# A decoder layer on one core: the feed-forward region of SBUF begins at another byte

## The reference

```python
x = x + 0.5 * swiglu(rmsnorm(x, n1), g1, u1, d1)          # 2048 -> 5632 -> 2048
h = rmsnorm(x, nm)
z = h @ w_in                                              # split by columns
x = x + concat([hgrn2_mix(z...), nsa_mix(z...)]) @ w_out  # 8 recurrent heads; 16 attention heads
x = x + mem_cross_attn(rmsnorm(x, nx), rmsnorm(mem, nmem), wq, wk, wv, wo)
x = x + 0.5 * swiglu(rmsnorm(x, n2), g2, u2, d2)
return rmsnorm(x, final_norm)
```

## The kernel before

| tile | where | remainder before |
| --- | --- | --- |
| `x`, `xT`, `w_raw`, `w_hi`, `w_lo`, `silu_gate`, `ff_hidden`, `kxT`, `ident` | ahead of `ff` | 128 |
| `ffT_hi`, `ffT_lo`, `mem_x`, `z_qf`, `z_ig`, `att`, level mask | in the region | 128 |
| `z_n` | in the region | 128 for tokens 0 to 127, 320 for the others |
| `qT`, `kT`, `prob0`, `probT` | in the region | 0 |
| `prob1` | in the region | 256 |
| `blk_hi`, `blk_lo` | in the region | 256 and 0 at the start, then steps of 264 bytes |

## Time and profile before

### The profile page before, as it was taken

How to read it: one execution, slowest core, us unless ns; L and a number is a source line. 1 busy time by engine, 2 the same in 40 slices (tenths; PEclk the granted TensorE clock), 3 DMA queues, 4 the chain that set the end, 5 groups by cost and what they waited for, 6 DMA issues and landing times.

```text
span 2136.0 us, 25561 instructions
## 1 busy us (share of the span) xinstructions
PE 2073.8 (97%) x9679; PEld 1727.3 (81%) x9679; DVE 1118.2 (52%) x1400; ACT 940.6 (44%) x1181; POOL 0.2 (0%) x4
## 2 busy tenths in 40 slices
PE   6999999999999999999999999799999999999997
PEld 5888888888888888878888987678888888888886
DVE  4544554445544445676567455454544545444444
ACT  6544444444444445454454244444444444444443
POOL 0000000000000000000000000000000000000000
PEclk8999999999999999999998699899999999999999
DMA  6666666666666566675540055256666666666563
GB/s 220 182 189 190 192 186 187 188 192 189 187 191 193 188 191 184 188 218 156 158 148 1 1 195 177 82 168 190 185 191 189 188 192 185 203 196 196 191 193 128
DMA packets 194343, 372.23 MB, mean 174 GB/s; under 512 B 12904, under 2 KB 15456, under 8 KB 194144
## 3 DMA queue, kind: packets, MB, share of 16 engines
q1 hardware_dynamic: 190176, 366.62, 57.0%
q10 hardware_dynamic: 4096, 4.64, 0.6%
HBM read 369.11 MB, written 2.10 MB: 174 GB/s over the span
## 4 chain that ended last, share of the span: by engine, by line
PE 94%; DVE 3%; ACT 2%; ACTq 1%; issue 1%; DVEq 0%
PE psum L1203 87%; PE psum L1214 2%; PE psum L1485 1%; PE psum L1439 1%; PE psum L1307 1%; PE psum L1407 0%; PE psum L1420 0%; ACT w_hi L423 0%; DVE xT_lo L781 0%; ACT xT_hi L446 0%; ACT silu_gate L453 0%; DVE att L1090 0%; DVE w_lo L745 0%; PE psum L1386 0%; ACTq L476 0%
## 5 line engine op out<-in xcount | busy, mean ns | idle before, releaser
L745 DVE TENSOR_TENSOR w_lo<-w_raw,w_hi 128x1024 fp32r<-128x1024 f32 x696 | 850.9, 1225 | 906.6 <-ACT w_hi L423 905.3
L423 ACT ACTIVATE w_hi<-w_raw 128x1024 fp32r<-128x1024 f32 x696 | 736.5, 1060 | 1028.6 <-PE psum L1203 1016.1
L1203 PE MATMUL psum<-w_hi,xT_hi 128*128 128x512 f32 (+1 forms) x1824 | 713.1, 391 | 7.5 <-DVE xT_lo L781 4.9
L1203 PE MATMUL psum<-w_hi,xT_lo 128*128 128x512 f32 (+1 forms) x1824 | 708.2, 388 | 0.0
L1203 PE MATMUL psum<-w_lo,xT_hi 128*128 128x512 f32 (+1 forms) x1824 | 708.1, 388 | 0.0
L1203 PEld LDWEIGHTS psum<-w_hi,xT_hi 128*128 128x128 f32 x1824 | 343.1, 188 | 79.9 <-DVE xT_lo L781 6.2
L1203 PEld LDWEIGHTS psum<-w_hi,xT_lo 128*128 128x128 f32 x1824 | 343.0, 188 | 70.6
L1203 PEld LDWEIGHTS psum<-w_lo,xT_hi 128*128 128x128 f32 x1824 | 343.2, 188 | 68.6
L1203 PE MATMUL psum<-w_hi,ffT_hi 128*128 128x512 f32 x928 | 364.8, 393 | 2.4 <-DVE ffT_lo L1170 2.4
L1203 PE MATMUL psum<-w_hi,ffT_lo 128*128 128x512 f32 x928 | 363.0, 391 | 0.0
L1203 PE MATMUL psum<-w_lo,ffT_hi 128*128 128x512 f32 x928 | 362.6, 391 | 0.0
(11 more groups left out here) (199 smaller groups left out, 707.4 us busy)
## 6 DMA issues: line engine op xcount, KB each, us to landing
w_raw<-in_g SPq DMA_DIRECT2D x176, 512.0 KB, 3.7
w_raw<-in_u SPq DMA_DIRECT2D x176, 512.0 KB, 3.7
w_raw<-in_d SPq DMA_DIRECT2D x176, 512.0 KB, 4.1
w_raw<-in_w_in SPq DMA_DIRECT2D x88, 512.0 KB, 3.7
w_raw<-in_w_out SPq DMA_DIRECT2D x32, 512.0 KB, 3.7
w_raw<-in_wk SPq DMA_DIRECT2D x8, 512.0 KB, 4.7
w_raw<-in_wv SPq DMA_DIRECT2D x8, 512.0 KB, 4.2
w_raw<-in_cw SPq DMA_DIRECT2D x8, 512.0 KB, 4.0
```

The costliest lines, as they stand in the source:

```text
L423: nc.scalar.activation(w_hi[:, slot], w_raw[:, slot], ACT.Copy).then_inc(w_hi_ready, 1)
L745: nc.vector.tensor_tensor(w_lo[:, slot], w_raw[:, slot], w_hi[:, slot].bitcast(F32), ALU.subtract)\
L1203: mm = nc.tensor.matmul(dst[:, t, 0:width], act_t, w[:, slot, kk, 0:width], start=(first and kk == 0 and n == 0), stop=(last and kk == KT_ ...
```

## The change

The region `ff` begins at the next multiple of 512 counted from byte 0 of the partition, where before it was counted from the start of `w_raw`. With `base` at 16,512 that moves `ff` from byte 135,808 (remainder 128) to byte 136,192 (remainder 0), and all tiles of the region with it, by 384 bytes. The tiles ahead of it stay.

```diff
         xt_end = at[0]
-        w_raw_at = at[0]
         w_raw = put("w_raw", [P, SLOTS, KT_U, NW], F32)
...
         w2 = put("w2", [P, 2, 2, DH], F32)
-        at[0] = (at[0] - w_raw_at + 511) // 512 * 512 + w_raw_at
+        at[0] = (at[0] + 511) // 512 * 512
         ff = at[0]
         ffT_hi = put("ffT_hi", [P, KF, SEQ], F32R)
         ffT_lo = put("ffT_lo", [P, KF, SEQ], F32R)
```

## The result

| | before | changed |
| --- | --- | --- |
| median, us | 2137.98 (2135.86 to 2140.46, 6 runs) | 2151.70 (2149.16 to 2154.13, 6 runs) |
| ratio | 1 | 1.0065, 95% interval 1.0052 to 1.0079 |
| span of the profiled execution, us | 2136.0 | 2149.2 |

What follows compares the result with a forecast made beforehand. PE's stream of matmuls was taken to bound the kernel. Terms of 0 + 0 + 0 on the profiled execution's 2137.88 us gave 2137.9 us; likeliest case 2133.6 to 2142.2, whole range 2133.0 to 2150.0.

Steps and rivals of the forecast that it cites:

- Term (a): The 2784 matmuls that take `ffT`: bounded between +12.0 and −37.3 us, taken as 0.
- R1: Matmuls on `ffT`: PE's two reads hinder each other at different remainders, +12.0 us (2149.9 us) or a part; chance 0.13.
- The bound: Price of unequal remainders for matmuls on `ffT`, from line 1307: 231 against 226.7 ns, 2784 × 4.3 ns = +12.0 us.
- R2: Matmuls on `ffT`: moving it away frees the 13.4 ns over the columns, up to −37.3 us (2100.6 us); chance 0.05.
- (b): ACT and DVE work on moved tiles: 0.5 us either way at most, taken as 0.
- (c): Transfers into the region (`mem_x`, `vec_rows`, level mask): 0.5 us once if not hidden, taken as 0.
- the prediction's signs: What the changed profile should show: ten steps on `ffT` in 2.27 us again, ACT's first work at 15.6 us.
- the prediction's estimate of a ninth: Transfers of `mem_x`: 8 transactions in place of 9 per 2,048-byte run at remainder 0, still hidden ahead of ACT's 15.63.
- The slack argument: Weight load before each matmul: 188 to 189 ns beneath 227, so lengthening costs nothing until 38 ns are used up.
- R3: Attention and recurrence stage moves as its tiles change remainders: 2137.3 to 2138.5 us, inside the no-difference case's 0.79.

Runs made afterwards that it cites:

- e1: Whole arena of the kernel before moved up by 384 bytes, so `xT`, the weights and `ffT` all begin at remainder 0: 2136.08 us, ratio 0.9996.
- e5: Against the kernel before, `w_hi`, `w_lo` and `ffT` moved to remainder 0, `xT` and `w_raw` left at 128: 2151.98 us in one execution.
- e10: Weights and `ffT` at remainder 0, `xT` and `w_raw` at 128, against the kernel before, timed over 4 runs: 2167.34 us, ratio 1.0142.
- e11: Against the kernel before, `xT` and `ffT` both put 128 bytes past the weights' remainder: 2182.99 us in one execution.
- e4: Against the kernel before, `xT` put 32 and `ffT` 64 bytes past the weights' remainder: 2186.01 us in one execution.
- e6: Against the kernel before, `xT` put 224 and `ffT` 192 bytes past the weights' remainder: 2178.04 us in one execution.

## Why the prediction was wrong

**What bounds the kernel** held: PE's stream of matmuls sets the end, and the whole loss is in it.

**Term (a), taken as 0, is the step that failed.** It is +15.2 us over the matmuls on `ffT` at full clock, or +13.4 by the busy time of their groups, which takes in the chance share of the clock. The place, the number of matmuls and the mechanism stood in R1, which had 0.13. I discarded it for two reasons, and neither carried. The first was that 230 ns occurs at equal remainders too. It does, but in units that follow other work of PE: in the trace of before, all but 8 of the distances over 228 ns are in the first unit (12 matmuls) behind such a break, none comes after the third, and in an unbroken stream at equal remainders the mean is 226.7. I compared a transient with a steady state. The second was that transposes with `prob` (0 and 256) and `silu_gate` (128) as the stationary operand take the same time. They do after the move as well, which brings `prob` into step with `ident`: from start to start at full clock 109 ns on either tile, before and after. But these are plain fp32 with 128 columns, and 109 ns is over twice the 53.3 of one column a cycle. What they show doesn't carry over to fp32r matmuls of 512 columns, and the prediction had said that it need not; whether the type or the width makes the difference no run separates. The prediction's chance for R1 should have been a good deal higher.

**The bound was too small.** Line 1307 gave +4.3 ns a matmul and +12.0 us; measured was +5.7 in the steady stream and +13.7 us by the medians, which ended 1.7 us above the range. Line 1307's stationary tiles step by 264 bytes, so that before they lie 128 to 248 bytes past the moving operand by the period of 256, never in step; its mean is over sixteen differences and not of the one asked. (One matmul of it was the very case that the prediction says is missing, remainder 0 against 128: the first on `blk_lo`.) The 66 columns aren't what costs. In the changed kernel the same tiles begin in step, and the first three pairs of them are at most 16 bytes out. The timeline of before, then of the changed kernel, ten starts each:

```profile
934.17 0.39 PE L1307 MATMUL psum<-w_hi,blk_hi 128*66 128x512 f32 x1
...
936.27 0.39 PE L1307 MATMUL psum<-w_hi,blk_hi 128*66 128x512 f32 x1
```

```profile
939.42 0.39 PE L1306 MATMUL psum<-w_hi,blk_hi 128*66 128x512 f32 x1
...
941.46 0.40 PE L1306 MATMUL psum<-w_hi,blk_hi 128*66 128x512 f32 x1
```

Nine steps take 2.10 us before, 233 ns each, and 2.04 after, 227 each. Nor was the row even before the change: the same three matmuls took from 680 to 705 ns, tile by tile (the last left out, which a break follows).

**R2** is refuted by eight differences, none under 226.7 ns. The 11 ns that stand between this and the 215.8 ns that are the isolated gap for 512 columns by the Trainium skill, page "TensorE: Matmul & The Clock Gate", section "Back-to-back issue gap", aren't to be had by a remainder.

**Terms (b) and (c)** were right in their size, 0. Exp on `prob`, now at 384 and 128, takes 499 and 390 ns, on `silu_gate` 498 and 392; `mem_x` lands in 6.7 us and `x` in 6.2, the 0.5 apart that they were the earlier trace rows. e1 has the whole region at the changed kernel's bytes and gave a ratio of 0.9996. One thing did move: ACT's table load comes at 15.29 us in place of 15.66 and its first work at 16.59 in place of 16.95 (the 15.6 of the prediction's signs is the table load). In all five traces in which `mem_x` begins at a multiple of 256 bytes (the changed kernel, e1, e5, e10, e11) the first work comes between 16.59 and 16.68 us, in the nine others between 16.95 and 17.06. The transfers differ in the same way: from the landing of the second quarter of `mem_x` to that of the third it is 1.24 to 1.25 us in the five and 1.35 to 1.37 in the nine; and for `x`, which only e1 puts on such a multiple, the step from the first quarter to the second is 1.26 us in e1 and 1.35 to 1.37 elsewhere. The direction is that of the prediction's estimate of a ninth, the size 8 to 9%, in one trace of each kernel. As the prediction said, it stays hidden.

**The slack argument** for the weight load was right in its words and beside the point: the load did stay at 189 ns in the mean with 38 ns to spare. The loss hardly shows in it: only under the longest distances (240 and 241 ns, about one in seven) does the next load take 192 ns, under the others 188.

**R3** didn't happen: the half-clock stretch is 58.0 us long in both kernels, 3.8 us later in the changed one.

## What to carry to other kernels

In a stream of fp32r matmuls with a weight load before each, the stationary tile and the moving tile should begin at the same remainder of 256 bytes; where that remainder lies doesn't matter. Here the blocks within each tile follow at multiples of 256 bytes, so that the start decides; where they don't (`blk_hi`, 264), each block has a difference of its own. A layout out of step cost 2.2 to 7.6 ns of 227 on each matmul here, and it shows in no wait and in no engine's idle time, only in the distance between starts, so compare that for each pair of tiles. Where a trace offers a natural experiment, ask whether it has the same data type and whether it is in the same state (steady or after a break) as the case in question; and read a row that is a mean over several cases case by case.

## What the runs showed of the hardware

- In step, a matmul of 512 columns starts every 226.7 ns at full clock, 13.3 ns over its columns. At half clock it doesn't have them: in the kernel before, seven steps from 27.66 to 30.65 us take 2.99 us, 427 ns each, which is 512 columns at 1.2 GHz (the granted clock from 27 to 31 us is 0.50):

```profile
27.66 0.63 PE L1203 MATMUL psum<-w_lo,ffT_hi 128*128 128x512 f32 x1
...
30.65 0.63 PE L1203 MATMUL psum<-w_hi,ffT_lo 128*128 128x512 f32 x1
```

- Out of step it is the same at half clock: in e11 seven steps from 27.31 to 30.29 us take 2.98 us, in e4 seven from 27.77 to 30.75 take 2.98, 426 ns each. The loss is one of full clock alone.
- The Trainium skill, page "TensorE: Matmul & The Clock Gate", section "Step-by-step: what each phase is for", gives PE two independent read ports, so that loading the next weights doesn't take bandwidth from the running matmul. These runs differ from that at full clock: with no other engine needed for it, the relative address of the two operands changes the rate by up to 3.4% (226.7 to 234.3 ns). What the two reads share wasn't found; that they meet in some bank or buffer with a period of 256 bytes is a guess and not shown.
- Out of step, the distances aren't random. At a difference of 128 (the changed kernel on `ffT`) they repeat over seven matmuls (228, 230, 233, 241, 232, 231, 232 ns; 1627 in all, ten times 13.3 over the columns), at 192 (e6 on `ffT`) over three (226, 229, 232).
- One program, unchanged, spent 30.7 or 58.0 us at half clock in the same stage, worth some 14 us of its time. A difference of that size between two single executions says nothing here.
